# FFN up and gate products of a two-block kernel: the high weight part takes x's high and low parts in one product of 512 columns

## What is computed

```python
# block 1
h = rms_norm(x, g_pre_ffn[l]) * (1.0 + scale_f) + shift_f
f = (jax.nn.silu(h @ w_ffn_gate[l]) * (h @ w_ffn_up[l])) @ w_ffn_down[l]
x = x + gate_f * rms_norm(f, g_post_ffn[l])
# block 2, 16 meta tokens stand ahead of the 256
g = causal_dwconv(h @ w_gate, w_conv)          # 3 taps along the tokens
f = (jax.nn.silu(g) * (h @ w_up)) @ w_down
```

## Time and profile before

| | us |
|---|---|
| median of 3 runs | 2462.29 (2458.07 to 2464.64) |
| profiled execution | 2455.74 |
| its span, first to last instruction | 2454.0 |
| TensorE busy | 2337.9 |
| VectorE busy | 1521.0 |
| ScalarE busy | 1047.3 |

### The profile page before, as it was taken

The page is one execution under the profiler, slowest core; times in us unless marked ns, Lnnn a source line. Parts: engine busy times, 40 slices in busy tenths (PEclk is TensorE's granted clock), DMA queues, the critical chain, the costliest instruction groups (busy, mean ns, idle before and its releaser), DMA issues.

```text
span 2454.0 us, 41724 instructions
## 1 busy us (share of the span) xinstructions
PE 2337.9 (95%) x16374; PEld 2177.6 (89%) x16374; DVE 1521.0 (62%) x1718; ACT 1047.3 (43%) x1225; POOL 107.9 (4%) x245
## 2 busy tenths in 40 slices
PE   3999989899999999999899999998999999999997
PEld 3999768899998899988799996798999978999986
DVE  7988688654454476644644995546566544556545
ACT  5463243544443344433545335445344333344333
POOL 0000011000001100001100000000000011000010
PEclk9999989999999999999999999699999999999999
DMA  9988759455555587745464551254555555555552
GB/s 394 422 326 332 316 205 387 162 188 188 188 174 203 173 296 283 271 158 193 135 187 159 188 171 52 70 172 138 189 180 179 188 179 196 182 180 177 184 187 103
DMA packets 162958, 506.49 MB, mean 206 GB/s; under 512 B 8096, under 2 KB 12496, under 8 KB 134048
## 3 DMA queue, kind: packets, MB, share of 16 engines
q1 hardware_dynamic: 161536, 500.28, 57.7%
q0 software_dynamic: 752, 3.48, 0.5%
q10 hardware_dynamic: 576, 1.44, 0.2%
HBM read 503.07 MB, written 2.10 MB: 206 GB/s over the span
## 4 chain that ended last, share of the span: by engine, by line
PE 87%; DVE 5%; DMA 4%; ACT 2%; issue 1%; ACTq 0%; DVEq 0%; SPq 0%
PE pb L560 23%; PE pb L547 18%; PE pb L549 18%; PE pb L548 18%; DMA raw<-w_in 3%; PE pb L526 1%; PE pb L527 1%; PE pb L528 1%; PE pb L910 1%; DMA sigc<-w_ada 1%; DVE x L1604 1%; PE pb L1111 1%; PE pb L677 1%; DVE wlo L489 1%; ACT xf L726 0%
## 5 line engine op out<-in xcount | busy, mean ns | idle before, releaser
L443 DVE TENSOR_TENSOR wlo<-raw,whi 128x1024 fp32r<-128x1024 f32 (+1 forms) x712 | 861.1, 1219 | 758.8 <-ACT whi L436 758.5
L436 ACT ACTIVATE whi<-raw 128x1024 fp32r<-128x1024 f32 (+1 forms) x712 | 745.4, 1054 | 1094.7 <-PE pb L549 725.8
L547 PE MATMUL pb<-xh,whi 128*128 128x256 f32 (+2 forms) x3760 | 1066.6, 284 | 7.1 <-DVE xl L736 3.0
L548 PE MATMUL pb<-xl,whi 128*128 128x256 f32 (+2 forms) x3760 | 1065.8, 283 | 0.0
L549 PE MATMUL pb<-xh,wlo 128*128 128x256 f32 (+2 forms) x3760 | 1065.3, 283 | 0.0
L547 PEld LDWEIGHTS pb<-xh,whi 128*128 128x128 f32 x3760 | 712.2, 189 | 8.6 <-ACT xf L726 3.5
L548 PEld LDWEIGHTS pb<-xl,whi 128*128 128x128 f32 x3760 | 713.2, 190 | 0.0
L549 PEld LDWEIGHTS pb<-xh,wlo 128*128 128x128 f32 x3760 | 711.9, 189 | 0.0
L560 PE MATMUL pb<-whi,stg 128*128 128x512 f32 x1664 | 452.3, 393 | 14.9 <-DVE wlo L443 5.4
L560 PEld LDWEIGHTS pb<-whi,stg 128*128 128x128 f32 x1664 | 315.0, 190 | 84.8 <-issue 6.4
L560 PE MATMUL pb<-wlo,stg 128*128 128x512 f32 x832 | 258.8, 392 | 0.0
...
## 6 DMA issues: line engine op xcount, KB each, us to landing
...
```

The costliest lines, as they stand in the source:

```text
L436: act.activation(to, src, ACT.Copy).then_inc(hi_ready, 1)
L443: dve.tensor_tensor(to, src, hi, ALU.subtract).then_inc(raw_done, 1)
L547: mm(o, whi[:, s, t], xh[:, k, c0:c1], start=(k == 0), stop=False)
L548: mm(o, whi[:, s, t], xl[:, k, c0:c1], start=False, stop=False)
```

## The change

`xh` and `xl` become the two parts of one tile `xx`, the same bytes in the same order. With `joint`, `chunk` makes for each tile one product of `whi` with both parts of x, 2 x 256 columns, into the whole bank, and one of `wlo` with `xh` into its first half. The bank then holds two halves that have still to be added. `joint` is on for both chunks of block 1 and for the up chunk of block 2.

The halves are added by VectorE, with a reduction over pairs of columns that lie 256 apart (`halves_of`). In `mid` of block 1 that addition writes `tb`, and ScalarE takes the sigmoid of `tb` and no longer of PSUM. In `end` of both blocks VectorE multiplies `tb` by the sigmoid, adds the halves of banks 4 to 7 into `hb`, and multiplies the two. The first slab's second half waits for that addition (`gated`) in place of `h_done`.

```diff
--- before.py
+++ after.py
@@ -296,17 +296,17 @@
     pb = stack.enter_context(nc.psum_tensor("pb", [P, 8, 512], F32))
-    (raw, whi, wlo, xh, xl, x, kc, colv, csil, mods, epsc, hst, stat, rstd), R0 = lay(base, [
+    (raw, whi, wlo, xx, x, kc, colv, csil, mods, epsc, hst, stat, rstd), R0 = lay(base, [
         ("raw", [P, RING, UNIT], F32),
         ("whi", [P, SLOTS, HALF], F32R),
         ("wlo", [P, SLOTS, HALF], F32R),
-        ("xh", [P, KT, T2], F32R),
-        ("xl", [P, KT, T2], F32R),
+        ("xx", [P, 2, KT, T2], F32R),
         ("x", [P, NT, D], F32),
...
 
+    xh, xl = xx[:, 0, :, :], xx[:, 1, :, :]
     (gateF, adaA, cosT, sinT), R1 = lay(R0, [("gateF", [P, D], F32), ("adaA", [P, D], F32),
@@ -531,7 +531,7 @@
     def chunk(u, w, b0, c0, c1, at=in_row, n0=0, nf=4, width=CW, i=0, nu=0, x_split=None,
-              behind=None):
+              behind=None, joint=False):
 
@@ -544,6 +544,11 @@
                     t = slice(kk * width + f * P, kk * width + (f + 1) * P)
+                    if joint:
+                        both = pb[:, b0 + f, :].rearrange("p (v n) -> p v n", v=2)
+                        mm(both, whi[:, s, t], xx[:, :, k, c0:c1], start=(k == 0), stop=False, skip_group_check=True)
+                        last = mm(o, wlo[:, s, t], xh[:, k, c0:c1], start=False, stop=(k == KT - 1), skip_group_check=True)
+                        continue
                     mm(o, whi[:, s, t], xh[:, k, c0:c1], start=(k == 0), stop=False)
@@ -601,6 +606,17 @@
 
+    def halves_of(b0):
+
+
+        return pb[:, b0:b0 + 4, :].rearrange("p b (v n) -> p b n v", v=2)
+
+    def gated_at(b, c):
+
+
+
+        return GATED0 + 3 * (c - CHUNK0) if b == 0 else GATED0 + 2 * (c - CHUNK0) + sum(GROUPS)
+
     def stage_tile(s, hi, lo, done, i=0, nk=0, nw=0):
@@ -801,9 +817,9 @@
 
-    FREE0, CHUNK0, CONVD0 = 2, 1, 12
-    START_FREE = [("bank_free", FREE0), ("convd", CONVD0)]
-    START_FREE += [(name, CHUNK0) for name in ("gated", "h_done", "ht_ready", "sig_done", "hth_done")]
+    FREE0, CHUNK0, CONVD0, GATED0 = 2, 1, 12, 3
+    START_FREE = [("bank_free", FREE0), ("convd", CONVD0), ("gated", GATED0)]
+    START_FREE += [(name, CHUNK0) for name in ("h_done", "ht_ready", "sig_done", "hth_done")]
     BF_WIN2 = FREE0
@@ -1040,7 +1056,7 @@
         up_cols = (0, SEQ) if b == 0 else (2, NQ)
-        gated = (lambda i: (sem("gated"), c + i)) if b == 0 else (lambda i: (sem("convd"), CONVD0 + 12 * (c - CHUNK0 - sum(GROUPS)) + 12 * i))
+        gated = (lambda i: (sem("gated"), GATED0 + 3 * (c - CHUNK0 + i) - 2)) if b == 0 else (lambda i: (sem("convd"), CONVD0 + 12 * (c - CHUNK0 - sum(GROUPS)) + 12 * i))
         for g, n in enumerate(GROUPS):
@@ -1048,11 +1064,11 @@
                 chunk(u, w, 0, *gate_cols, at, 0, i=i, nu=nu, x_split=None if g else 8 * b,
-                      behind=behind)
+                      behind=behind, joint=b == 0)
                 pe.wait_ge(sem("h_done"), c + i)
                 if g:
                     pe.wait_ge(sem("part_done"), 4 * (2 * b + g))
-                chunk(u, w + 8, 4, *up_cols, at, 4, i=i, nu=nu)
+                chunk(u, w + 8, 4, *up_cols, at, 4, i=i, nu=nu, joint=True)
 
@@ -1071,7 +1087,7 @@
             for j in range(4):
-                slab(u + j, w + 2 * j, st + 2 * (j + 1), j % 2, j == 0, freed=None if j else (sem("h_done"), c))
+                slab(u + j, w + 2 * j, st + 2 * (j + 1), j % 2, j == 0, freed=None if j else (sem("gated"), gated_at(b, c)))
             with pe.Fori(1, n - 1) as i:
@@ -1296,9 +1312,9 @@
                 if b == 0:
-                    act.wait_ge(used, w + 8 + i * 16)
+                    act.wait_ge(sem("gated"), GATED0 + 3 * (c - CHUNK0) + 1 + i * 3)
                     at_least(act, sem("ht_ready"), c + i)
-                    act.activation(hb[:, :, :], pb[:, 0:4, 0:SEQ], ACT.Sigmoid).then_inc(sem("sig_done"), 1)
+                    act.activation(hb[:, :, :], tb[:, :, :], ACT.Sigmoid).then_inc(sem("sig_done"), 1)
                 else:
@@ -1611,12 +1627,11 @@
                 at_least(dve, sem("h_done"), c + i)
+                dve.wait_ge(used, w + 8 + i * 16)
                 if b == 0:
-                    dve.wait_ge(sem("sig_done"), c + 1 + i)
-                    settle(dve)
-                    dve.tensor_tensor(tb[:, :, :], pb[:, 0:4, 0:SEQ], hb[:, :, :], ALU.mult).then_inc(sem("gated"), 1)
+                    dve.tensor_reduce(tb[:, :, :], halves_of(0), AX.X, ALU.add)\
+                       .then_inc(sem("gated"), 1)
                     return
-                dve.wait_ge(used, w + 8 + i * 16)
                 for tap in range(3):
@@ -1629,12 +1644,15 @@
             def end(i, w=w, c=c):
-                if b == 1:
-                    dve.wait_ge(sem("sig_done"), c + 1 + i)
-                    dve.tensor_tensor(tb[:, :, :], tb[:, :, :], hb[:, :, :], ALU.mult).then_inc(sem("gated"), 1)
-                dve.wait_ge(sem("gated"), c + 1 + i)
+                per, gated = 3 - b, gated_at(b, c)
+                dve.wait_ge(sem("sig_done"), c + 1 + i)
+                dve.tensor_tensor(tb[:, :, :], tb[:, :, :], hb[:, :, :], ALU.mult).then_inc(sem("gated"), 1)
+                dve.wait_ge(sem("gated"), gated + per - 1 + i * per)
                 dve.wait_ge(used, w + 16 + i * 16)
-                dve.tensor_tensor(hb[:, :, :], tb[:, :, :], pb[:, 4:8, 0:SEQ], ALU.mult).then_inc(sem("h_done"), 1)
+                dve.tensor_reduce(hb[:, :, :], halves_of(4), AX.X, ALU.add)\
+                   .then_inc(sem("gated"), 1)
+                dve.wait_ge(sem("gated"), gated + per + i * per)
+                dve.tensor_tensor(hb[:, :, :], hb[:, :, :], tb[:, :, :], ALU.mult).then_inc(sem("h_done"), 1)
                 dve.wait_ge(sem("hth_done"), c + 1 + i)
```

## The result

| | before | after |
|---|---|---|
| median, us | 2461.68 (14 runs) | 2470.04 (14 runs, 2465.70 to 2480.47) |
| ratio, 95% interval | | 1.0037 (1.0027 to 1.0046) |
| profiled execution, us | 2455.74 | 2470.00 |

The changed kernel is slower by 0.37%, some 9 us (6.6 to 11.3). No change was forecast. The two profiled executions lie 14.3 us apart.

The account below looks back on a forecast made before the run. TensorE, busy 95% of the span, was taken to set the time wherever it has no gap. The terms -21.1 + 0.3 + 6.7 + 8.1 + 6.0 summed to 0.0 us, so the forecast was 2462 us, range 2449 to 2479.

Parts of the forecast that it names:

- What goes: TensorE's chunks in both FFNs: 2112 products fall away, each saving its surplus over its columns, 21.1 us in all.
- products that go, first FFN: First FFN, both chunks: 8.6 ns saved per tile, 1408 times, 12.1 us.
- products that go, second FFN: Second FFN, up chunks only: 12.8 ns saved per tile, 704 times, 9.0 us.
- plain transitions: Between pairs of the first FFN without an ada sum: TensorE waits 0 to 0.1 us in each of six, 0.3 us.
- ada waits: First FFN's second group, where VectorE has a 2.35 us ada sum: TensorE waits 2.2 us at three transitions, 6.7 us.
- first slabs: First slab behind each group: TensorE waits longer for banks 4 to 7, by 2.3, 3.6 and twice 1.1 us, 8.1 us.
- clock: TensorE after waits: the granted clock can fall to 1.2 GHz for a stretch, adding 6.0 us, bounds 0 and 12.
- rival 2: VectorE's addition is slower than one element a cycle; at 4.4 us it costs 42 us, giving 2504 us; chance 0.07.
- Number 4: TensorE's removed products: surplus belongs to columns or the jump; 5 to 9 us saved, 2476 us; chance 0.06.

Follow-up runs that it names:

- one_run: Changed kernel, but the joint product's 512 moving columns lie in one run, without the jump between x's two parts; 2474.29 us, a single run.
- near_pieces: Changed kernel, but the joint product's two pieces of 256 columns come from neighbouring tiles of xh, 64 bytes apart; 2477.17 us, a single run.

## Where the forecast was right and where it was wrong

**The step that failed: the term "What goes".** It took the joint product at 226.7 ns from the 512-column row of the down product, "a direct measurement of that size", and at 231.0 in the second FFN. It is 232.6 and 236.3, and the neighbour has 0.7 ns more in the first FFN. Worth per tile: 3 x 117.65 - 350.9 = 2.0 ns where 8.6 stood, and some 8 (0.50 us in 64 tiles) where 12.8 stood. A part of the second miss is a reading: 121.9 ns for a product of the second FFN's up chunks came from the starts of VectorE's splits, and by TensorE's own starts it is 121.2, so that the odd start costs 3.6 ns and not 4.2.

| term, us | forecast | measured |
|---|---|---|
| products that go, first FFN | -12.1 | 11 x -0.27 = -3.0 |
| products that go, second FFN | -9.0 | 11 x -0.50 = -5.5 |
| plain transitions | +0.3 | 0 |
| ada waits | +6.7 | 3 x 2.1 = +6.2 |
| first slabs | +8.1 | +8.1 |
| clock | +6.0 | about +4.3 |
| sum | 0.0 | about +10 |

Measured is the sum of what the traces show at these places; the ratio gives +9. Taken whole, the first FFN is 13.3 us longer (747.5 to 760.8) and the second 3.3 us shorter (757.4 to 754.1), +10.0 too. The ada waits are counted by how much later the starts come, some 0.2 us over the idle time. For the clock: two stretches of 3.4 us after the ada waits, 1.7 us each, and one of 6.8 us that begins at 1100.5, 1.6 us ahead of the first product, where there were 3.4 us before: 5.2 / 2 less 3.4 / 2, some 0.9. The one at 2346 was there before too. Of the 14.2 us between the two spans the rest lies in code that was not touched: the first FFN product starts 1.4 us later, and the second block's mixer takes 2.8 us longer, with 3.4 us more at the half clock.

**What held.** The addition took 2.29 us, in 22 and in 11 instructions, as forecast from the reductions of the earlier trace rows (1753 and 182 ns are 1504 elements apart, 1.045 ns each, which puts 2048 elements at 2.29 us), and with no surcharge for the step of 1 KB in PSUM. Groups by line and shape of the changed kernel:

```profile
L1652 DVE TENSOR_REDUCE hb<-pb 128x1024 f32<-128x2048 f32 x22 | 50.4, 2292 | 0.8
...
L1632 DVE TENSOR_REDUCE tb<-pb 128x1024 f32<-128x2048 f32 x11 | 25.1, 2284 | 0.0
```

So rival 2 fell. The Trainium skill, page "SBUF — State Buffer", section "Door 1: The DMA port swizzle", gives PSUM lines of 8 bytes. It states the penalty for leaving a line where it speaks of SBUF, and for PSUM it names matmuls; the forecast carried it over to VectorE's addition, where these 33 instructions, which leave the line with each element, show none. The chain behind the addition held to 0.01 us and the slab waits to 0.1; the ada waits came 0.1 to 0.3 us shorter, because TensorE, slower than counted, arrives later. That the plain transitions had no wait is luck in part: their cover was 0.06 us as counted, and it is the slower joint product that brings TensorE 0.2 us later.

**The clock** was near in size (4.3 for 6.0) and wrong in place: two ada waits of 1.9 us cost a stretch, while the slabs at 729 and 1982, with 3.2 us of idle time, cost none. Idle time alone does not decide, and no run shows what does.

**The rivals.** Number 4, "what goes is worth less than 8.6 ns", with a chance of 0.06, is what happened in mechanism: it named 5 to 9 us saved, and 8.5 were. It got its low chance from "235.3 and 226.7 ns for the same 512 columns", a comparison across two stages, the very step that failed. Its reasons (a jump between x's parts, a surplus of the columns) are not borne out: the jump was excluded by one_run and near_pieces, and no run shows that a chunk's surplus goes with its columns. Its time of 2476 was too high, because it kept the full clock term and waits. The measured 2470 lies inside the forecast's range; that is no merit of the sum, since the term it rests on was off by 12.6 us. The Trainium skill, page "TensorE: Matmul & The Clock Gate", section "Back-to-back issue gap", gives N/2.4 + 2.5 ns for a warm product; the forecast had set it aside, and it holds in neither stage: by it 256 columns take 109.2 ns, against 117.6 in a chunk and 120.0 in the down product. That a product less was worth 2.0 ns in the first FFN, near the 2.5 ns of the Trainium skill, was therefore no sign that its rule holds here.

The sign of the error follows: with -8.5 in place of -21.1 the forecast's own sum would have been +12.6, slower.
